# Expert sum of a two-layer MoE model: ScalarE scales the expert rows, GpSimd adds them, VectorE adds the residual

## The reference

```
y = jnp.zeros((T, D)).at[row_tok].add(yb * row_gate[:, None])   # two rows of 1024 per token
h = _layer_norm(DN_ALPHA * h + ff, ln2_g[li], ln2_b[li])        # ff is y, DN_ALPHA = 4 ** 0.25
```

## Time and profile before

| | before |
|---|---|
| median of 3 runs | 5266.57 us |
| lowest and highest | 5254.99 and 5270.5 us |
| span of the profiled execution | 5259.3 us |
| busy share PE, DVE, ACT, POOL | 92%, 63%, 41%, 25% |
| the stage in layer 0 | about 1908 to 2011 us |
| the stage in layer 1 | about 3877 to 3982 us |

### The profile page before, as it was taken

How to read it: one execution, slowest core, us unless ns; L and a number is a source line. 1 busy time by engine, 2 the same in 40 slices (tenths; PEclk the granted TensorE clock), 3 DMA queues, 4 the chain that set the end, 5 groups by cost and what they waited for, 6 DMA issues and landing times. The chain is left out here.

```text
span 5259.3 us, 128868 instructions
## 1 busy us (share of the span) xinstructions
PE 4816.5 (92%) x56566; PEld 4148.9 (79%) x56566; DVE 3308.0 (63%) x5011; ACT 2130.2 (41%) x3887; POOL 1325.3 (25%) x952
## 2 busy tenths in 40 slices
PE   7989999999799958989999999799969988999999
PEld 6888888887688848878888887588857767788887
DVE  5336666558788874345655558788876365662662
ACT  2323333333288842433333333288844143232331
POOL 0013333232244510012323322244421100122221
PEclk9999999999899978989999999899989989999999
DMA  5410101013367664310101013367662002333332
GB/s 144 145 50 19 32 20 32 19 37 110 118 238 271 242 186 118 101 52 20 32 19 31 19 41 107 127 233 267 250 193 79 21 1 85 92 98 120 112 99 102
DMA packets 383086, 536.31 MB, mean 102 GB/s; under 512 B 136482, under 2 KB 306594, under 8 KB 354466
## 3 DMA queue, kind: packets, MB, share of 16 engines
q1 hardware_dynamic: 339714, 488.61, 29.1%
q0 software_dynamic: 41472, 34.21, 2.1%
q10 hardware_dynamic: 1344, 5.24, 0.3%
HBM read 573.01 MB, written 122.09 MB: 132 GB/s over the span
## 5 line engine op out<-in xcount | busy, mean ns | idle before, releaser
L281 PE MATMUL ps<-w_hi,xbT 128*128 128x512 f32 x1536 | 502.5, 398 | 17.4 <-DVE w L2710 17.3
L281 PE MATMUL ps<-hT,w_in 128*128 128x416 f32 (+1 forms) x2736 | 497.1, 340 | 8.6 <-DVE hT L2939 8.6
L281 PEld LDWEIGHTS ps<-hT,w_in 128*128 128x128 f32 x2736 | 460.7, 197 | 34.7 <-issue 19.3
L2710 DVE TENSOR_TENSOR w<-w,w_hi 128x2048 fp32r<-128x2048 f32 x192 | 429.9, 2277 | 2.2 <-ACT w_hi L2667 2.2
L1556 POOL TENSOR_TENSOR lm<-Ab,consts 116x416 f32<-116x416 f32 x240 | 255.3, 1071 | 591.2 <-PE ps L281 315.7
L2667 ACT ACTIVATE w_hi<-w 128x2048 fp32r<-128x2048 f32 x192 | 359.1, 1936 | 0.0
L281 PEld LDWEIGHTS ps<-w_hi,xbT 128*128 128x128 f32 x1536 | 289.4, 188 | 85.9 <-DVE w L2710 26.6
L281 PE MATMUL ps<-w,xbT 128*128 128x512 f32 x768 | 300.4, 391 | 0.0
L281 PE MATMUL ps<-v,pT 104*104 104x128 f32 (+1 forms) x2176 | 271.3, 281 | 27.5 <-issue 27.5
L2741 DVE TENSOR_TENSOR w<-w,w_hi 128x2048 fp32r<-128x2048 f32 x96 | 223.4, 2327 | 97.1 <-ACT w_hi L2703 97.1
L281 PEld LDWEIGHTS ps<-v,pT 104*104 104x104 f32 (+1 forms) x2176 | 249.7, 179 | 39.0 <-issue 32.5
(11 more groups left out here) (454 smaller groups left out, 11475.7 us busy)
## 6 DMA issues: line engine op xcount, KB each, us to landing
w<-in_moe_w_dram SPq DMA_DIRECT2D x192, 1024.0 KB, 12.4
w_gate<-in_w_gate_dram SPq DMA_DIRECT2D x44, 512.0 KB, 3.8
w_up<-in_w_up_dram SPq DMA_DIRECT2D x44, 512.0 KB, 3.9
w_down<-in_w_down_dram SPq DMA_DIRECT2D x44, 512.0 KB, 3.2
w_in<-in_w_in_dram SPq DMA_DIRECT2D x36, 512.0 KB, 4.6
ys<-t_ys SPq DMA_DIRECT2D x20, 832.0 KB
t_h<-x SPq DMA_DIRECT2D x30, 416.0 KB
w_out<-in_w_out_dram SPq DMA_DIRECT2D x24, 512.0 KB, 7.6
```

The costliest lines, as they stand in the source:

```text
L281: made = e.matmul(out, a, b, start=start, stop=stop)
L2710: e.tensor_tensor(w.lo, w.x, w.hf, ALU.subtract).then_inc(*P.c("moe_dve").tick(li, "w13", b, k))
```

## The change

ACT no longer scales h. It waits for the load of the expert rows instead and multiplies both by their gates, in place, in the slot where h was scaled (two instructions for one). POOL gets a new program `combine_pool`: for each tile it waits for ACT's second product and adds the two rows into the first. DVE waits for the load of h and for POOL's sum, and makes one multiply-add, h = h * ALPHA1 + sum. The buffer of the expert rows is given back by that one multiply-add. The low parts of the weight blocks, which POOL did before in one go, now stand between the additions: in layer 0 one behind each of the additions of tiles 2, 3 and 4, in layer 1 two behind each of tiles 2 to 5. POOL's new count shares the semaphore of an earlier stage.

```diff
+SHARED["com_pool"] = "clo_pool"
...
     def load_sum(i):
         if i >= NY:
-            e.wait_ge(*P.c("com_dve").at(li, i - NY, "y", 1))
+            e.wait_ge(*P.c("com_dve").at(li, i - NY, "x"))
...
         i = t[0]
         if i is not None:
-            x = m.hx[i % NS][0:C, :]
-            e.wait_ge(*P.d(f"com_h{i % NS}_in").at(li, i))
-            e.activation(x, x, ACT.Copy, scale=ALPHA1).then_inc(*ac.tick(li, i, "h"))
+            e.wait_ge(*P.d(f"com_y{i % NY}_in").at(li, i))
+            for kx in range(2):
+                y = m.yv[i % NY][0:C, kx, :]
+                e.activation(y, y, ACT.Copy, scale=P.gates[0:C, kx, i:i + 1]).then_inc(*ac.tick(li, i, "y", kx))
...
+def combine_pool(e, P, li):
+    m = P.com[li]
+    for i in range(NT):
+        y = m.yv[i % NY][0:C]
+        e.wait_ge(*P.c("com_act").at(li, i, "y", 1))
+        e.tensor_tensor(y[:, 0, :], y[:, 0, :], y[:, 1, :], ALU.add).then_inc(*P.c("com_pool").tick(li, i, "y"))
+        if li == 0 and i in (2, 3, 4):
+            n = i - 2
+            half_lo(e, P, 1, n, lo_taker(P, n))
+        if li and i in (2, 3, 4, 5):
+            for k in range(2 * i - 4, 2 * i - 2):
+                values_lo(e, P, 0, k, P.c("val_pool"))
...
             x = m.hx[i % NS][0:C, :]
-            e.wait_ge(*ac.at(li, i, "h"))
-            e.wait_ge(*P.d(f"com_y{i % NY}_in").at(li, i))
-            for kx in range(2):
-                if kx:
-                    e.wait_ge(*dv.last())
-                e.scalar_tensor_tensor(x, m.yv[i % NY][0:C, kx, :], P.gates[0:C, kx, i:i + 1], x, ALU.mult, ALU.add
-                                       ).then_inc(*dv.tick(li, i, "y", kx))
-            e.wait_ge(*dv.at(li, i, "y", 1))
+            e.wait_ge(*P.d(f"com_h{i % NS}_in").at(li, i))
+            e.wait_ge(*P.c("com_pool").at(li, i, "y"))
+            e.scalar_tensor_tensor(x, x, ALPHA1, m.yv[i % NY][0:C, 0, :], ALU.mult, ALU.add).then_inc(*dv.tick(li, i, "x"))
+            e.wait_ge(*dv.at(li, i, "x"))
             combine_norm(P, li, i).stats_dve(e)
...
-        if li == 0:
-            front_early_pool(e, P, 1)
-    values_early_pool(e, P)
+        combine_pool(e, P, li)
```

More of the change, by code:

```diff
@@ L2959, in combine_pe @@
                 pass
-COMBINE = ("com_in", "com_dve", "com_act", "com_pe") + tuple(f"com_y{s}_in" for s in range(NY)) + tuple(
+COMBINE = ("com_in", "com_dve", "com_act", "com_pool", "com_pe") + tuple(f"com_y{s}_in" for s in range(NY)) + tuple(
     f"com_h{s}_{x}" for s in range(NS) for x in ("in", "out"))
```

## The result

| | before | after |
|---|---|---|
| median, first session (6 runs each) | 5262.43 us (5251.5 to 5270.5) | 5277.55 us (5272.55 to 5283.0) |
| ratio | | 1.0033, 95% interval 1.0023 to 1.0043 |
| median, second session (15 and 5 runs) | 5260.67 us | 5283.57 us |
| ratio | | 1.0046, 95% interval 1.0032 to 1.0060 |
| span of the profiled execution | 5259.3 | 5270.7 |

The changed kernel is slower by 15 us in the first session and by 23 us in the second; weighted by the inverse squares of their widths the two ratios make 1.0037, some 20 us. (The recorded ratio isn't the quotient of the two medians, which would be 1.0029 and 1.0044. The first interval reaches from +12 to +23 us.) The forecast was +20.8 us and 5287. The lines that follow are of the first profiled execution of the changed kernel.

The account below looks back on a forecast made before the run. PE is busiest overall, but in the two stages it waits for DVE's low part of tile 7. Start, rounds, low parts and late slice, less old stalls and waits, made +11.4 and +9.4 us: 5287 us, range 5268 to 5296.

Parts of the forecast that it names:

- The steady round: DVE, one tile's bn_aggr end (M) to the next: waiting for POOL's sum, +1.02 us per round, +9.2 per layer.
- The first rounds: First two rounds of a layer, without low part: DVE's norm and POOL's addition meet likewise, also +1.02 us each.
- The start: Before DVE's first multiply-add of a layer: ACT's products and POOL's addition come first, +3.4 us per layer, uncovered.
- The low parts: POOL's low parts behind additions go first, hold up DVE's multiply-add: +6.15 us layer 0, +4.0 layer 1; old stalls go.
- The late slice: Layer 1, PE's first product: last weight slice now behind tile 5's addition, making ACT about 1.5 us late, once.
- The sums: Terms added per layer: +11.4 us in layer 0, +9.4 in layer 1, together +20.8.
- The narrow range: Whole-kernel time under the likeliest forecast, 5280 to 5292 us; an addition between 2.0 and 2.5 us moves it by 4.
- DVE ahead of the low parts: DVE's multiply-add slips in before POOL's low parts, which then run beside unstalled statistics; 5278 us, chance 0.2.
- No mutual stall: POOL's addition does not block DVE; a round changes by +0.02 us, time 5261.5, within 0.3%; chance 0.12.
- PE cold in layer 1: PE idles about 13 us before the last slice, next product up to 10 us; time say 5294, chance 0.1.
- POOL ahead of L330 in the steady round: POOL's addition gets in before DVE's norm: round 9.35 not 9.54 us, total 5284; shares the forecast's chance 0.52.
- The rule beside the rows: Holder of the shared port pair keeps it whole instruction: stalls and additions count POOL's full row, some 3 us more, 5291.

Follow-up runs that it names:

- OLD = 4: Against the kernel before: tiles 0 to 3 made the old way, tiles 4 to 9 added on GpSimd one tile ahead; 5249.38 us, ratio 0.9979.

## Why the prediction was right

The mechanism, the order of the engines and nearly every size held. The single steps:

- **The steady round**, forecast 9.54: measured 9.54 to 9.60. ACT's pair 2.20, measured 2.18. The addition of 2.34 is 2.33 alone, and its row 3.38 beside L330. It ends 2.24 after L330 (forecast 2.20). Multiply-add at M + 6.70, measured + 6.78.
- **The first rounds**: here the sum was off by a third of a microsecond in layer 0. The round to M(1) grew by 0.68, not 1.02, because the round of before was 0.36 us longer than it need be (DVE stood idle for 0.46 us ahead of L324; in layer 1 this idle time is missing, and the same round grew by 1.04). The meeting itself is as forecast: without a low part of a tile L330 begins 1.51 us after M, POOL's addition stands for its last stretch only (1929.06, row of 2.51), and it ends 2.2 us after L330. The round to M(2) grew by 3.08, as forecast (1.02 and 2.05).
- **The start**, forecast 3.4: measured 3.48 and 3.43.
- **The low parts**: POOL got in first, by 0.14 us, as the earlier trace rows had led me to expect; the stall is 2.04 in layer 0 (forecast 2.05) and 0.96 in layer 1 (forecast 1.0). Moving them behind the multiply-add gave back 6.1 of the 6.15 us in layer 0. In layer 0 the wait of 3.28 for h of tile 4 is gone, so the round to M(4) is 2.25 shorter.
- **The late slice**, forecast 1.5: measured 2.0 (the round to M(6) is 11.57 where its neighbours are 9.56). PE waited 6.65 us for the slices. By the rows some 1.4 of the 2.0 are the lower clock, on three matmuls (1.65 for 0.97) and eight transposes (1.59 for 0.88).
- **The sums**: 11.2 for 11.4 and 9.6 for 9.4. The total of the stages is 20.8, as forecast to the tenth. That it agrees so closely is luck: errors of a few tenths cancel, and against the second trace of before the total is 18.1.
- **The time**: 5287 was forecast, and 5277.6 and 5283.6 were measured. Of the 9.8 us by which the first lies below 5287.4, 4.1 come from the base: the forecast was set on 5266.57, a median of three runs, and six runs gave 5262.43. The other 5.7 are in the difference itself (15.1 for 20.8, which lies inside the first interval), and this the second session (22.9) does not bear out. The narrow range of 5280 to 5292 holds the second median only. The first profiled pair shows the same thing: 7.8 us between the stages and 5.6 behind them were given back, 3.9 ahead of them lost, and the 7.8 turned round when both kernels were run again. Behind the stages before took 1287.0 us and again 1282.4, after 1281.4 and again 1281.7. The last gated products were forecast at 2013.5 and 3993 and stand at 2017.22 and 3989.41: the first stage began 3.9 us later, and the second had the 7.8 us back.
- **The chances**: the ratios, 1.0033 and 1.0046, lie above the bound of 0.3% between "slower" and "same", the first barely and with an interval across it; the forecast of +0.4% implies as much. The range of 5268 to 5296 holds both medians.

**The rivals.** DVE ahead of the low parts: the rows show POOL ahead, each of the seven times. No mutual stall: refuted by L330's 2.73 us beside an addition that nobody waits for. In the changed kernel itself that row is at its 1.28 us and the stall is POOL's. PE cold in layer 1: it came, but small. The granted clock was 0.50 around the last slice, and the product behind it took 7.33 us and not up to 10 (before 5.82). PE stood idle again for 5.64 us ahead of the product of 3970.23, so the long product held nobody up, and only some 1.4 us ahead of it reached M(6). POOL ahead of L330 in the steady round: it arrives 0.14 us behind, by 0.02 from what I had worked out. So narrow an order is close to luck, but the forecast had a place for either.

**The rule beside the rows.** DVE's multiply-add ended 2.04 us late beside a low part whose row is 2.33 long, and the addition ended 2.24 after L330. The stall is 0.1 to 0.3 us shorter than POOL's instruction each time. The Trainium skill, "SBUF — State Buffer", section "Who interferes with whom", has the holder of the shared port pair keep it for the whole instruction, which would have made 5291; the rows bear out its main statement, the mutual exclusion, and its order of issue, and stay a little under its full length. Why, no run shows.

## What to carry to other kernels

Before work is moved from VectorE to an idle GpSimd, look at what VectorE runs at that moment. Where the sum was needed in the same round and met two-input instructions over SBUF, a round here lost 2.4 us to save 1.3: some 1.4 by the wait for the sum and 1.0 by the exclusion. Beside statistics or subtractions from PSUM it was free. A sum that is needed in the round in which it is made lies on the path with all its hops, so pipeline it by one tile first: the same offload went from +20 us to -11 us when it was made a tile ahead, laid beside the statistics, and left out where late loads set the pace; some 8 of these 31 us are the low parts, which were moved behind the multiply-adds at the same time (8.4 us of the stages in the run that moved them alone). Don't queue GpSimd's next work directly behind the instruction that VectorE waits for. And a stall that ends in a wait for a load is no gain when it is removed.

## What the runs showed of the hardware

- Both directions of the exclusion were seen with L330: POOL's addition of 2.33 us became 3.38 behind it, and its own 1.28 us became 2.73 behind POOL's addition in one buffer. `bn_stats` (0.69 and 0.68), a DVE subtraction of PSUM and SBUF (1.09 the pair, in the round from 1956.10 with OLD = 4, beside an addition that began at 1956.16) and ACT's products (2.19) kept their lengths beside POOL.
- The addition of 104x1024 f32 takes 1.22 us on DVE and 2.34 on POOL; on POOL with both inputs and the output in one buffer it takes 1.89.
- DVE's multiply-add is 1.22 to 1.23 us long with a constant as factor, where the one with a column of gates took 1.28.
- PE's granted clock was 0.50 (the lower level) after 6.65 us of idling ahead of the last slice in layer 1; three matmuls took 1.65 us there and 0.97 in the kernel before.
- Two executions of the same program differed by 8 us in a stretch of 1870 us in which PE is busy for 94% of the time, and the slower one had drops of the granted clock where the other was at the full level; the whole spread of a kernel is some 20 us, about the effect under study. A single pair of spans (here +11.4 us) can't tell +15 from +21; lengths of the stage, which repeat to 0.1 us in the changed kernel but only to 2.7 us (both stages) in the kernel before, can tell them better.
